# Diffusion trunk step on one core: filter inputs loaded first, projections on alternating banks beside the modulations, spectra and input tiles side by side

## What is computed

```python
def modulate(x, shift, scale):
    return rms_norm(x) * (1.0 + scale) + shift          # input of layer 0

def adaln(cvec, w_mod_l, b_mod_l):
    m = jax.nn.silu(cvec) @ w_mod_l + b_mod_l           # shift, scale, gates
    return jnp.split(m[:, None, :], 6, axis=-1)

def implicit_filters(...):                              # for layer 1
    hid = jnp.sin(freq * (z @ wf1 + bf1))
    hid = jnp.sin(freq * (hid @ wf2 + bf2))
    filt = (hid @ wf3).astype(jnp.float32)
    return filt * jnp.concatenate([decay, decay], axis=-1)
```

## Time and profile before

| | |
|---|---|
| median of 3 runs | 1831.93 us (1830.75 to 1832.19) |
| the profiled execution itself | 1831.89 us |
| its span in the profile | 1830.1 us |
| PE matmul busy | 1724.7 us, 94% |
| DVE / ACT / POOL busy | 846.3 / 578.1 / 92.2 us |
| read and written in memory | 160.61 and 5.87 MB |

### The profile page before, as it was taken

How to read it: one execution, slowest core, us unless ns; L and a number is a source line. 1 busy time by engine, 2 the same in 40 slices (tenths; PEclk the granted TensorE clock), 3 DMA queues, 4 the chain that set the end, 5 groups by cost and what they waited for, 6 DMA issues and landing times.

```text
span 1830.1 us, 28580 instructions
## 1 busy us (share of the span) xinstructions
PE 1724.7 (94%) x11636; PEld 1591.2 (87%) x11636; DVE 846.3 (46%) x1499; ACT 578.1 (32%) x891; POOL 92.2 (5%) x68
## 2 busy tenths in 40 slices
PE   4899996798999999999999999898999999999997
PEld 2489985677999999999999997576999999999997
DVE  4624238565633333333337345854544333433344
ACT  3432455253432112211215344234342212211223
POOL 0000027000000000000000202000000000000012
PEclk9899998898999999999999999999999999999998
DMA  9245304002534253425325213000332133224112
GB/s 299 87 131 185 110 28 154 7 24 81 150 93 138 81 150 95 135 81 150 108 80 167 79 47 95 1 24 1 87 98 69 47 92 92 58 58 115 55 36 83
DMA packets 235894, 167.91 MB, mean 92 GB/s; under 512 B 7387, under 2 KB 231857, under 8 KB 235410
## 3 DMA queue, kind: packets, MB, share of 16 engines
q1 hardware_dynamic: 234992, 165.76, 30.4%
q10 hardware_dynamic: 802, 0.73, 0.2%
HBM read 160.61 MB, written 5.87 MB: 91 GB/s over the span
## 4 chain that ended last, share of the span: by engine, by line
PE 88%; DVE 7%; ACT 2%; issue 1%; POOL 1%; ACTq 1%; DMA 0%; DVEq 0%; POOLq 0%
PE ub L902 12%; PE ua L902 12%; PE ua L904 12%; PE ua L903 12%; PE ub L903 12%; PE ub L904 12%; PE pm L832 2%; PE ua L1115 2%; PE ub L1115 1%; PE pt L1138 1%; PE pm L1138 1%; PE ua L1126 1%; PE ua L818 1%; DVE sct L2071 1%; DMA negt<-in_c_negt 0%
## 5 line engine op out<-in xcount | busy, mean ns | idle before, releaser
L1663 ACT ACTIVATE whi<-raw 128x2048 fp32r<-128x2048 f32 (+2 forms) x106 | 148.4, 1400 | 686.9 <-PE ub L904 347.2
L1938 DVE TENSOR_TENSOR wlo<-raw,whi 128x2048 fp32r<-128x2048 f32 (+2 forms) x123 | 215.6, 1752 | 48.6 <-ACT whi L1455 19.8
L902 PE MATMUL ua<-in_a_high,whi 128*128 128x384 f32 (+1 forms) x736 | 230.2, 313 | 2.3 <-DVE in_a_rest L1979 1.9
L902 PE MATMUL ub<-in_b_high,whi 128*128 128x386 f32 (+1 forms) x720 | 226.6, 315 | 5.8 <-DVE in_b_rest L2205 3.1
L904 PE MATMUL ua<-in_a_high,wlo 128*128 128x384 f32 (+1 forms) x736 | 228.3, 310 | 0.0
L903 PE MATMUL ua<-in_a_rest,whi 128*128 128x384 f32 (+1 forms) x736 | 227.9, 310 | 0.0
L902 PE MATMUL ua<-in_b_high,whi 128*128 128x386 f32 (+1 forms) x720 | 225.5, 313 | 0.0
L904 PE MATMUL ub<-in_b_high,wlo 128*128 128x386 f32 (+1 forms) x720 | 224.5, 312 | 0.0
L903 PE MATMUL ub<-in_b_rest,whi 128*128 128x386 f32 (+1 forms) x720 | 224.1, 311 | 0.0
L904 PE MATMUL ua<-in_b_high,wlo 128*128 128x386 f32 (+1 forms) x720 | 223.5, 310 | 0.0
L903 PE MATMUL ua<-in_b_rest,whi 128*128 128x386 f32 (+1 forms) x720 | 222.9, 310 | 0.0
(11 more groups left out here) (563 smaller groups left out, 2722.5 us busy)
## 6 DMA issues: line engine op xcount, KB each, us to landing
raw<-in_w_ffn_in SPq DMA_DIRECT2D x88, 512.0 KB, 5.1
modw<-in_w_mod SPq DMA_DIRECT2D x38, 1024.0 KB, 5.5
raw<-in_w_ffn_out SPq DMA_DIRECT2D x32, 512.0 KB, 3.8
raw<-in_w_in_even SPq DMA_DIRECT2D x10, 1024.0 KB, 7.7
raw<-in_w_in_odd SPq DMA_DIRECT2D x7, 1024.0 KB, 5.5
raw<-in_w_ffn_out SPq DMA_DIRECT2D x16, 384.0 KB, 3.3
mod_first<-in_w_mod SPq DMA_DIRECT2D x5, 1024.0 KB, 12.8
mod_tail<-in_w_mod SPq DMA_DIRECT2D x4, 1024.0 KB, 4.8
```

The lines of the kernel that those rows point to most:

```text
L902: pe.matmul(dst, wh, xh, start=first, stop=False)
L1663: act.activation(whi[s][:, 0:width], raw[s][:, 0:width], ACT.Copy).then_inc(w_hi, 1)
L1938: dve.tensor_tensor(wlo[s][:, 0:width], src[s][:, 0:width], whi[s][:, 0:width].bitcast(F32), ALU.subtract).then_inc(w_lo, 1)
```

## The change

Loads: the six filter inputs are split. The first layer's weights, its input and three vectors of 64 numbers (`fvec`, a column each) come first on ACT's queue, then the two conditioning vectors in a tile of their own (`crow`), then `brow`, then the rest of the filter inputs under a semaphore `f_w`. The other eleven vector rows move to SP's queue, behind `perm` and ahead of `wgate` and of the first weights of layer 0. `vrow` is turned after unit 0.

PE: the first filter layer waits for its five loads alone; the second stands one round earlier; tile 0 is projected in round 6; projections use banks `pm`/`pt` and `ua` in turn, the last one `ub`, beside the last modulations. Spectra wait tile by tile and use eight banks.

DVE: combines of tiles 0 to 2 stand between the last modulations; `w_rest(0)` stands after the last combine.

ACT: the second sine and the first two decays move into rounds 6 and 7; two spectra are copied first, then one after each input tile.

```diff
+        fvec = sb("fvec", [64, 3])
+        crow = ta("crow", [16, P])
+        fdec = [sb("fdec0", [P, HY], at=sb_at["crow"] + 512), sb("fdec1", [P, HY], at=phase_at + 55808)]
+        SPECTRUM = (0, 2, 4, 6, 1, 3, 5, 7, 8, 9)
+        SPECTRUM_BANKS = (2, 5, 6, 7, 0, 1, 3, 4, 6, 7)
+        FILTER_BANKS = ((6, 7), (0, 1), (6, 7), (0, 1), (3, 4))
...
# SP, after perm, ahead of wgate
+            sp.wait_ge(s_zero, 1)
+            def vec(name, src, rows):
+                r = VEC[name]
+                sp.dma_start(vrow[r:r + rows, :], src).then_inc(s_rows, 16)
+            for name, rows in (("b_gla_gate_f", 2), ("b_gla_gate_b", 2), ("g_gla_norm", 1), ("g_gqa_q", 1),
+                               ("g_gqa_k", 1), ("g_mla_q", 2), ("g_mla_kv", 1), ("hy_skip", 4), ("b_hy_conv", 12)):
+                vec(name, i_[name].rearrange("a (r p) -> (a r) p", p=P), rows)
+            vec("g_final", ...)
+            vec("w_hy_conv", ...)
...
# PE
                 if n:
                     pe.wait_ge(f_sin, 1)
                 else:
-                    pe.wait_ge(f_ld, 16 * 6)
-                    pe.wait_ge(vec_c, 2)
+                    pe.wait_ge(f_ld, 16 * 5)
...
             def filter_spectrum(n):
-                if n >= 6:
+                if n >= 8:
                     pe.wait_ge(g_ev, n - 5)
-                b = banks[n % 6]
+                pe.wait_ge(f_ok, 2 if n < 4 else 4 if n < 8 else TT)
+                b = banks[SPECTRUM_BANKS[n]]
...
-                if k == 4:
+                if k == 3:
+                    pe.wait_ge(f_w, 16 * 4)
                     filter_layer(1)
-            pe.wait_ge(f_sin, 2)
+                if k == 6:
+                    filter_project(0)
             pe.wait_ge(xt_c, KD)
-            for t in range(TT):
-                filter_project(t)
-                if t < 2:
-                    first_mm(6 + t)
-                if t < 3:
-                    first_tr(5 + t)
-                if t == 1:
-                    norm_sum(0)
-            pe.wait_ge(f_ok, TT)
+            filter_project(1)
+            first_tr(5)
+            norm_sum(0)
+            first_mm(6)
+            filter_project(2)
+            first_tr(6)
+            filter_project(3)
+            first_mm(7)
+            first_tr(7)
+            pe.wait_ge(rs_ready, 1)
+            filter_project(4)
             pe.wait_ge(s_const, 80)
-            for n in range(10):
+            pe.wait_ge(m_red, MOD_FIRST)
+            filter_spectrum(0)
+            filter_spectrum(1)
+            pe.wait_ge(f_fr, 3)
...
                 if n < 2:
-                    pe.wait_ge(g_ev, 9 + n)
+                    pe.wait_ge(g_ev, (6, 8)[n])
...
+                if n == 0:
+                    pe.wait_ge(s_rows, 16 * 11)
+                    pe.wait_ge(g_ev, 10)
+                    pe.transpose(pt[:, 0:P], vrow[:, :], ident[:, :]).then_inc(vec_t, 1)
...
# ACT
-            act.wait_ge(s_zero, 1)
-            for name, rows in (("c", 8), ("b_gla_gate_f", 2), ...):
-                vec(name, ...)
             act.dma_start(wf1[:, :], f("w_filt1")).then_inc(f_ld, 16)
             act.dma_start(zf[:, :], i_["c_z"]).then_inc(f_ld, 16)
+            for n, name in enumerate(("b_filt1", "filt_freq", "b_filt2")):
+                act.dma_start(fvec[:, n:n + 1], i_[name].rearrange("a p -> p a")).then_inc(f_ld, 16)
+            act.dma_start(crow[0:8, :], i_["c"].rearrange("a (r p) -> (a r) p", p=P)).then_inc(s_vec, 16)
+            act.dma_start(crow[8:16, :], i_["c_ctx"].rearrange("(r p) -> r p", p=P)).then_inc(s_vec, 16)
+            act.wait_ge(s_zero, 1)
+            act.dma_start(brow[0:96, :], ...).then_inc(s_vec, 16)
+            act.dma_start(wf2[:, :], f("w_filt2")).then_inc(f_w, 16)
+            act.dma_start(wf3[:, :], f("w_filt3")).then_inc(f_w, 16)
+            act.dma_start(delta[:, :], i_["c_delta"].to_broadcast([P, HY])).then_inc(f_w, 16)
+            act.dma_start(negt[:, :], i_["c_negt"]).then_inc(f_w, 16)
...
             for k in range(KD):
-                if k == 3:
-                    filter_sine(0)
+                if k in (2, 6):
+                    filter_sine(k // 6)
+                if k == 7:
+                    act.wait_ge(f_w, 16 * 4)
+                    filter_decay(0)
+                    filter_decay(1)
...
+            filter_decay(2)
+            norm_scale(0)
             w_high(0, 0, KD * EVEN_COLS[0][1])
-            norm_scale(0)
-            for t in range(2, TT):
+            for t in range(3, TT):
                 filter_decay(t)
...
-            for n in range(4):
-                spectrum_out(n)
+            spectrum_out(0)
+            spectrum_out(1)
             for k in range(KD):
...
                 ins.then_inc(h_hi, 1)
-                if k < 3:
-                    spectrum_out(4 + 2 * k)
-                    spectrum_out(5 + 2 * k)
+                spectrum_out(2 + k)
...
# DVE
+            filter_combine(0)
+            first_reduce(5)
+            first_row(6)
+            filter_combine(1)
+            first_reduce(6)
+            first_row(7)
+            filter_combine(2)
+            first_reduce(7)
+            filter_combine(3)
+            filter_combine(4)
+            w_rest(0, 0, KD * EVEN_COLS[0][1])
```

More of the change, by code:

```diff
@@ L787, in _ @@
         def _(pe):
-            pe.wait_ge(s_vec, 16 * 18)
-            pe.transpose(pt[:, 0:P], vrow[:, :], ident[:, :])
-            pe.transpose(pt[:, P:2 * P], brow[:, :], ident[:, :]).then_inc(vec_t, 1)
             def filter_layer(n):
@@ L846, in norm_sum @@
                 pe.wait_ge(ssq_added, KD * (q + 1))
-                pe.matmul(pm[:, 0:T1], ones[:, :], ssq[:, 0:T1], start=True, stop=True)
-                pe.matmul(pt[:, 0:T2], ones[:, :], ssq[:, T1:T], start=True, stop=True).then_inc(ssq_sum, 1)
+                a, b = (pm, pt) if q else (ub[:, 0], ub[:, 1])
+                pe.matmul(a[:, 0:T1], ones[:, :], ssq[:, 0:T1], start=True, stop=True)
+                pe.matmul(b[:, 0:T2], ones[:, :], ssq[:, T1:T], start=True, stop=True).then_inc(ssq_sum, 1)
             def first_mm(n):
@@ L1430, in square, with filter_decay @@
                 act.activation(sq[:, n % 2], x[:, n], ACT.Square, scale=D ** -0.5).then_inc(sq_ready, 1)
+            def filter_decay(t):
+                if t >= 2:
+                    act.wait_ge(f_fr, t - 1)
+                act.activation(fdec[t % 2][:, :], delta[:, :], ACT.Exp, scale=negt[:, t:t + 1]).then_inc(f_dec, 1)
             for k in range(KD):
-                if k == 3:
-                    filter_sine(0)
+                if k in (2, 6):
[4 more added lines that the diff above has]
+                    filter_decay(1)
                 act.wait_ge(xt_t, k + 1)
@@ L1438, in _ @@
                 square(0, k)
-            filter_sine(1)
-            def filter_decay(t):
-                if t >= 2:
-                    act.wait_ge(f_fr, t - 1)
-                act.activation(fdec[:, t % 2], delta[:, :], ACT.Exp, scale=negt[:, t:t + 1]).then_inc(f_dec, 1)
-            filter_decay(0)
-            filter_decay(1)
             def norm_scale(q):
                 act.wait_ge(ssq_sum, q + 1)
-                inv_sqrt(rstd[:, 0], ((slice(0, T1), pm[:, 0:T1]), (slice(T1, T), pt[:, 0:T2]))).then_inc(rs_ready, 1)
+                a, b = (pm, pt) if q else (ub[:, 0], ub[:, 1])
+                inv_sqrt(rstd[:, 0], ((slice(0, T1), a[:, 0:T1]), (slice(T1, T), b[:, 0:T2]))).then_inc(rs_ready, 1)
             def w_high(u, s, width):
@@ L1939, in w_rest @@
                                   ALU.subtract).then_inc(w_lo, 1)
-            for t in range(TT):
-                if t == 2:
-                    w_rest(0, 0, KD * EVEN_COLS[0][1])
-                if t < 2:
-                    first_row(6 + t)
-                if t < 3:
-                    first_reduce(5 + t)
-                filter_combine(t)
+            filter_argument(0)
+            dve.wait_ge(vec_t, 1)
+            dve.tensor_copy(bmod[:, :], ub[:, 2, 0:96]).then_inc(vec_c, 1)
+            for k in range(KD):
+                if k >= 1:
+                    add_square(0, k - 1)
+                if k >= 2:
+                    first_row(k - 2)
+                if k >= 3:
+                    first_reduce(k - 3)
+                if k == 4:
+                    filter_argument(1)
+            add_square(0, KD - 1)
+            filter_combine(0)
[9 more added lines that the diff above has]
+            w_rest(0, 0, KD * EVEN_COLS[0][1])
             def mod_finish(layer, m0, m1):
```

85 lines of the change are left out of this document (38 added, 47 removed).

## The result

| | before | after |
|---|---|---|
| median of 5 runs | 1831.93 us (1830.75 to 1832.36) | 1819.1 us (1813.54 to 1821.21) |
| the profiled execution | 1831.89 us | 1817.06 us |
| its span | 1830.1 us | 1815.3 us |

The ratio is 0.9926, with an interval of 0.9908 to 0.9944: faster by 0.7%. The changed kernel was run in two more sets: medians 1814.5 and 1820.4 us. Over all 14 executions the median is 1817.2 us, and they reach from 1813.1 to 1824.3, a spread of 11.2 us. The later executions of the kernel before lie between 1830.4 and 1834.6, a spread of 4.2; the experiments come back to this. One further execution of that kernel took 2168.1 us at a mean granted clock of 0.746, a slow state, and is left out of every comparison.

What follows compares the result with a forecast made beforehand. Almost the whole program is PE multiplying, so unit 1's start decides: 11.2 us from the later stretch and 3.8 from the earlier, sum 15.0, take 1831.89 to 1816.9, say 1817.0 us; range 1811.5 to 1822.0.

Steps and rivals of the forecast that it cites:

- The later stretch: From `hbuf` of tile 0 to unit 1's first product: 19.0 us instead of 30.2, a gain of 11.2 us.
- The second argument: On DVE amid the modulations: starts at 26.3, takes 5.24 us, and the fifth product follows at 32.9.
- The step that was mis-sized: PE behind the second argument: fifth product at half clock, 1.93 us, projection 2.2, sixth product 1.07; first combine at 41.0.
- The combines: DVE from the first combine at 41.0, sharing with PE, through the last and w_rest: `hbuf` at 60.7.
- DVE's wait for the eighth product: Between DVE's combines: done at 47.6, DVE stands 2.7 us until the eighth row is copied at 50.3.
- the term for PE's clock at unit 1's start: At unit 1's start: three us at half clock spared or added, an unknown of 1.5 us.
- The signs of being wrong: Unit 1 starting after 85, or the time differing from unit 1's shift by more than 2 us.
- its unknowns for PE's clock: Parts of the range: 2 us for second argument and clock, 1.5 us for PE's clock at unit 1's start.
- Row loads hold SP's queue: Eleven row loads, 2.92 us each, delay the first weights to 76.4; unit 1 at 104.8, 1842 us; chance 0.04.
- Head not held: PE at full clock, products as weights land, first combine near 37: `hbuf` at 54.4, 1810.6 us; chance 0.07.
- Half clock through the spectra: Ten spectra at half clock take 31 us from 53.5; unit 1 at 89.4, 1826.6 us; chance 0.05.
- Given back behind unit 1: Spill and next weights end about 93, covered until 97; at twice the time 6 us given back, 1823; chance 0.04.

Runs made afterwards that it cites:

- The experiments on either half: Changed kernel with ACT's old order of copies (four first, then two per tile): 1822.8 us; changed kernel with every spectrum waiting for the fifth combine: 1820.4 us.
- the order alone: Kernel before with only the new order of spectra, banks and copies, all spectra still waiting for all five tiles: 1824.4 us, ratio 0.9957.
- one gap filled: Changed kernel with five unused products in PE's gap ahead of the fifth modulation product: 1813.7 us, ratio 0.9892.
- two gaps filled: Changed kernel with four unused products ahead of the first modulation product and five ahead of the fifth: 1814.2 us, ratio 0.9908.
- early argument with gaps filled: Changed kernel, second filter layer ahead of the second modulation product, its argument earlier on DVE, unused products ahead of first and third: 1811.6 us, 0.9895.
- its variant with the eighth product first: Changed kernel, second filter layer and argument earlier, unused products in both gaps, eighth modulation product ahead of tile 3's projection: 1810.5 us, 0.9889.

## Why the prediction was right, and where it was off

**The later stretch** was right in mechanism and size: 19.1 us against 19.0, from `hbuf` to unit 1. No `in_a_rest` waits over 0.16 us. The sentence that spectra are no longer ahead of anything DVE waits for holds with 2.07 us to spare, and only since they start before the last combines (55.33, counted at 53.5). The experiments on either half show that neither gives more than 7.1 us in the changed kernel, and the order alone only 5.0 in the kernel before.

**The second argument** began at 26.64, against 26.3, and the fifth product at 33.17, against 32.9. Layer one ran at 10.13 instead of near 8, waiting for `fvec`, which no row had priced, and its argument ended at 17.9 instead of 15. That was covered, as the weights held the first product until 18.39.

**The step that was mis-sized** is "I take the same here: product 1.93 ... projection of tile 0 2.2 ... sixth product 1.07". I gave the half clock one product and priced what follows at full clock. The fifth product still ran at 1.07 and the half clock lay on what came behind: two halves of the projection 3.7 us, turns 1.26, the sixth product 1.67. From the fifth product's start to the sixth's end it was 8.3 us instead of 6.6. The first combine started at 43.07 instead of 41.0. The count allowed 0.9 us for the half clock (1.93 instead of 1.07) from the second argument to the first combine; with the gap filled this piece is 13.2 us in two profiles instead of 16.4, so it cost 3.2. That makes the clock the cause and not DVE's order. The earlier trace rows had held the warning: 0.50 over 3 us from 38 to 41, and the turns at 40.68 in the earlier trace rows took 1.03. The Trainium skill, "TensorE: Matmul & The Clock Gate", in its section on why this matters for kernels, advises against idle gaps between bursts of products; the trace agrees, with the granted clock at 0.52 over 34 to 41 behind the gap of 3.76 us.

**The combines** ran nearly as counted. DVE's wait for the eighth product was there, 1.83 us. The prediction's 2.7 reach from 47.6 to 50.3 and so contain the copy of the row; by its own count the product ends at 49.9, a wait of 2.3. From the first combine to `hbuf` it was 19.0 us instead of 19.7, so 0.7 of the 2.1 us were taken up; `hbuf` came at 62.08 against 60.7 and unit 1 at 81.19 against 79.7.

**Unit 1 to the end.** The copy behind unit 1 moved from 112.24 to 97.17, 15.1 us, 1.5 more than unit 1's start. Before, PE ran at half clock shortly behind the start of unit 1; from its windows:

```profile
96.00:99.00 3.00, 3.00 (x14) 3.00 (x13) 2.29 (x1) 0.23 (x1) 0.00 (x0) 0.50 0.93 311
```

Now the clock is 1.00 from 80 to 99 us, and the unit lasts 16.0 us instead of 17.5. This is the term for PE's clock at unit 1's start, and it fell to the good side. It happens to cancel the 1.5 us by which unit 1 was late, so that the profiled execution came out at 1817.06 against 1817.0. The exactness is luck; the median of the same five runs is 2 us higher, within the range.

**The signs of being wrong**, unit 1 after 85 or a time that differs from its shift by more than 2 us, are absent from this profile (81.19, and 14.8 us for a shift of 13.5), but not from the two later ones of the same kernel. In the second set's, the time is 17.3 us under the 1831.89 for a shift of 12.9; in the third's, unit 1 starts at 86.07. So the account holds for the schedule, and its unknowns for PE's clock, 2 us up to the first combine and 1.5 at unit 1, were too small for single executions.

**The rivals.** *Row loads hold SP's queue*: they take 3.4 us together, and the weights issued at 40.33 land 5.2 us later. The nearest price was that of ACT's queue for the same rows, 0.42 us at most. The Trainium skill, "DMA: Bandwidth & Descriptors", gives its fixed cost in the section on the anatomy of one DMA for transfers issued by gpsimd; that cost isn't seen in what a load holds of SP's queue here, 0.23 to 0.34 us. *Head not held*: the head as it is was held. Taking the second argument out of the middle brought unit 1 forward by 4.1 us, but filling the gaps with the argument left in its place brought 3.9, and both together only 4.4 (76.78). So the two are not separate gains: what the argument's place costs is in the main the half clock behind the gap that it makes. At full clock the first combine came at 39.23, not near 37. *Half clock through the spectra*: the first spectrum took 3.38 us, with the clock at 0.50 over 56 to 58, and the others followed every 1.7 us, at full clock. *Given back behind unit 1*: the weights behind the spill landed at 90.2, at the last 2.7 us before unit 1's end counted with `whi` and `wlo` (1.92 and 2.30); covered, and nearer than the 4 us I had.

## What to carry over

Price a half-clock stretch over everything that follows the gap until the clock returns (here 7 us), not over the first product, and look for each gap in which the new order leaves PE idle. When two engines wait for each other's leftovers, moving one order alone may give less than half: work out the stretch with each half undone. A head that is tightened may show variations that a slack head hid, and one profiled execution may not have the median's course, so measure such a change by several sets of runs.

## What was not expected

- Products that nobody reads brought unit 1 forward in the trace, by keeping the clock at 1.00. In time this is not settled. With one gap filled it is 1813.7 us beside 1820.4 in the same set, the ratios' intervals just apart; but its ratio, 0.9892, can't be told from the 0.9903 of the changed kernel's second set. With two gaps filled the ratio is 0.9908, and the changed kernel didn't run in that set.
- The clock's column shows 1.00 at the program's beginning, where the lengths of the products are those of half clock, in the kernel before too: five turns took 1.33 us there at 20.72 and 0.77 at 25.18.
- A wait of about 2 us for weights, 17 us into the program, was followed in three profiles by 7 to 10 us of half clock; in the changed kernel's third set unit 1 then starts 4.9 us later (86.07 against 81.19). The length of the wait isn't the whole of it: ahead of unit 1, PE was idle 2.40 us in the early argument with gaps filled and stayed at full clock, and idle 2.39 us in its variant with the eighth product first, and fell. What else the clock goes by stays open.
